# HGRN layers: state products placed between the tiles of the next values' unit, and a rearranged end of the last head pair

## The reference

```python
q, f_pre, i_in, g = split(x @ w_in)
f = lb + (1 - lb) * sigmoid(f_pre);  k = 1 - f
b = cumsum(log f)                                   # within a block
o_intra = tril(q_r @ k_r.T) @ v                     # the same block
for each block:                                     # the state goes from block to block
    o = q_inter @ state
    state = state * decay + k_state.T @ v
o = rmsnorm(o_intra + o_inter) * silu(g)
y = o @ w_out
```

## Time and profile before

| | us |
|---|---|
| median of 3 runs | 2880.5 |
| lowest and highest | 2877.11, 2885.57 |
| the profiled execution's own time | 2878.74 |
| its span, first to last instruction | 2877.0 |
| PE busy in the span | 2665.0 (93%) |
| DVE, ACT, POOL busy | 1697.5, 1300.9, 196.2 |
| TensorE's mean granted clock | 0.968 of full speed |

### The profile page before, as it was taken

How to read it: one execution, slowest core, us unless ns; L and a number is a source line. 1 busy time by engine, 2 the same in 40 slices (tenths; PEclk the granted TensorE clock), 3 DMA queues, 4 the chain that set the end, 5 groups by cost and what they waited for, 6 DMA issues and landing times.

```text
span 2877.0 us, 45279 instructions
## 1 busy us (share of the span) xinstructions
PE 2665.0 (93%) x18569; PEld 2486.4 (86%) x18569; DVE 1697.5 (59%) x1894; ACT 1300.9 (45%) x1625; POOL 196.2 (7%) x331
## 2 busy tenths in 40 slices
PE   5879989799999898999999799999799999898998
PEld 4769988699999797998989699899789999898898
DVE  6667865665555665556556655555655555575654
ACT  3644346443533554434444543444453453464543
POOL 2210002000100111000000000000010000011000
PEclk9989999899999899999999999999899999998999
DMA  8638844375555333655554355465355555443453
GB/s 289 212 125 312 333 142 147 134 243 187 190 185 187 125 118 128 201 183 179 190 175 140 109 194 185 163 204 185 130 184 187 185 181 182 153 147 103 162 190 117
DMA packets 349161, 509.52 MB, mean 177 GB/s; under 512 B 9055, under 2 KB 302118, under 8 KB 344934
## 3 DMA queue, kind: packets, MB, share of 16 engines
q1 hardware_dynamic: 343216, 493.42, 50.9%
q0 software_dynamic: 3808, 11.66, 1.1%
q10 hardware_dynamic: 2006, 2.60, 0.3%
HBM read 505.80 MB, written 1.84 MB: 176 GB/s over the span
## 4 chain that ended last, share of the span: by engine, by line
PE 83%; DVE 7%; ACT 5%; issue 2%; DMA 1%; POOL 1%; DVEq 0%; ACTq 0%; POOLq 0%
PE B L526 18%; PE B L527 18%; PE B L528 18%; PE Y L526 9%; PE Y L528 8%; PE Y L527 8%; ACT w_hi L1253 2%; DVE w_lo L1758 2%; DVE h_lo L1821 1%; ACT junk L1264 1%; DVE tmp L1783 1%; DVE x L1786 1%; DMA raw<-in_w_ada 1%; DMA raw<-in_w_in 0%; ACT h_hi L1303 0%
## 5 line engine op out<-in xcount | busy, mean ns | idle before, releaser
L1758 DVE TENSOR_TENSOR w_lo<-raw,w_hi 128x2048 fp32r<-128x2048 f32 x425 | 966.7, 2276 | 466.1 <-ACT w_hi L1253 464.8
L1253 ACT ACTIVATE w_hi<-raw 128x2048 fp32r<-128x2048 f32 x425 | 804.7, 1897 | 582.6 <-PE B L528 531.7
L526 PE MATMUL B<-h_hi,w_hi 128*128 128x256 f32 x3712 | 1053.5, 284 | 10.7 <-DVE h_lo L1821 5.9
L527 PE MATMUL B<-h_lo,w_hi 128*128 128x256 f32 x3712 | 1049.0, 283 | 0.0
L528 PE MATMUL B<-h_hi,w_lo 128*128 128x256 f32 x3712 | 1048.6, 282 | 0.0
L526 PEld LDWEIGHTS B<-h_hi,w_hi 128*128 128x128 f32 x3712 | 706.1, 190 | 16.8 <-issue 13.4
L527 PEld LDWEIGHTS B<-h_lo,w_hi 128*128 128x128 f32 x3712 | 703.5, 190 | 4.1 <-issue 0.5
L528 PEld LDWEIGHTS B<-h_hi,w_lo 128*128 128x128 f32 x3712 | 704.9, 190 | 0.0
L526 PE MATMUL Y<-w_hi,a_hi 128*128 128x512 f32 x812 | 319.3, 393 | 0.9 <-DVE M L2279 0.5
L528 PE MATMUL Y<-w_hi,a_lo 128*128 128x512 f32 x812 | 318.6, 392 | 0.0
L527 PE MATMUL Y<-w_lo,a_hi 128*128 128x512 f32 x812 | 317.6, 391 | 0.0
(11 more groups left out here) (306 smaller groups left out, 2673.2 us busy)
## 6 DMA issues: line engine op xcount, KB each, us to landing
raw<-in_ffn_w_in SPq DMA_DIRECT2D x176, 1024.0 KB, 5.1
raw<-in_ffn_w_out SPq DMA_DIRECT2D x88, 1024.0 KB, 4.9
raw<-in_w_gate_up SPq DMA_DIRECT2D x44, 1024.0 KB, 5.1
raw<-in_hgrn_w_in SPq DMA_DIRECT2D x32, 1024.0 KB, 5.3
raw<-in_w_ada SPq DMA_DIRECT2D x24, 1024.0 KB, 5.3
M<-in_w_ada SPq DMA_DIRECT2D x24, 1024.0 KB, 7.5
raw<-in_w_down SPq DMA_DIRECT2D x22, 1024.0 KB, 5.0
raw<-in_w_in SPq DMA_DIRECT2D x14, 1024.0 KB, 5.5
```

Source lines behind the costliest of these rows:

```text
L526: pe.matmul(o, lh, rh, start=first, stop=False)
L527: pe.matmul(o, lh, rl, start=False, stop=False)
L1253: act.activation(w_hi[st.n % RING][:, 0:n], raw[st.r % RING][:, 0:n], ACT.Copy).then_inc(unit_rounded, 1)
L1758: dve.tensor_tensor(w_lo[s][:, 0:n], raw[st.r % RING][:, 0:n], w_hi[s][:, 0:n].bitcast(F32), ALU.subtract).then_inc(unit_split, st.step("" ...
```

## The change

Three things are moved; no instruction is added or removed, and no size is changed.

1. On PE, the state product of pairs 0, 1 and 2 moves from the end of `scores` to the middle of the next pair's v unit, between its first and second tile. That of pair 3 stays where it was.
2. On DVE, at the end of the layer, masks and state of pair 3 come first, then `turned(0)`, and the split of the third `w_out` unit after these.
3. On PE, `turn(1)` moves from behind `out_pair(0)` into it, between its first and second tile.

```diff
-            def moving(os, name, n, lh, ll, kt, stride):
+            def moving(os, name, n, lh, ll, kt, stride, halfway=None):
                 hi, lo = unit()
                 for t in range(NT):
+                    if halfway and t:
+                        halfway()
                     for c, (o, w) in enumerate(os[t]):
...
                     mm.then_inc(tensor_step, st.step(f"{p}.far{c}"))
+
+                def state_product(c):
+                    bs = 3 if c == 3 else 7
                     pe.wait_ge(scalar_step, st.at(f"{p}.ksT{c}"))
                     pe.wait_ge(scalar_step, st.at(f"{p}.v{c}.ev"))
...
                 def out_pair(u):
+                    def before(t, i):
+                        if t == 1 and i == 0 and u == 0:
+                            turn(1)
+                        if i == 0:
+                            pe.wait_ge(vector_step, st.at(f"{p}o.h{t}.{u // 2}"))
+
...
-                    moving_unit(2, "v", c)
+                    moving_unit(2, "v", c, lambda: state_product(c - 1))
                     outputs(c - 1)
                     moving_unit(3, "g", c)
                 scores(3)
+                state_product(3)
                 turn(0)
                 outputs(3)
                 out_pair(0)
-                turn(1)
                 out_pair(2)
...
+                masked(3)
+                state(3)
+                turned(0)
                 lo(2 * D)
-                masked(3)
-                turned(0)
-                state(3)
                 gated(3)
                 normed(3)
                 turned(1)
```

More of the change, by code:

```diff
@@ L960, in stationary_unit, with moving_unit @@
                     stationary(B[u], f"{p}.{e}{c}", p if c == 0 and e == "f" else None)
-                def moving_unit(u, e, c):
+                def moving_unit(u, e, c, halfway=None):
                     if c:
                         pe.wait_ge(st.sem_of(f"{p}.{e}{c - 1}.ev"), st.at(f"{p}.{e}{c - 1}.ev"))
-                    moving([[(B[u][:, t * CH:t * CH + CH], CH)] for t in range(NT)], f"{p}.{e}{c}", CH, h_hi, h_lo, KD, CH)
+                    moving([[(B[u][:, t * CH:t * CH + CH], CH)] for t in range(NT)], f"{p}.{e}{c}", CH, h_hi, h_lo, KD, CH, halfway)
                 def scores(c):
@@ L1037, in out_pair @@
                 def out_pair(u):
+                    def before(t, i):
[3 more added lines that the diff above has]
+                            pe.wait_ge(vector_step, st.at(f"{p}o.h{t}.{u // 2}"))
                     into_y_pair(p, (f"{p}.out{u}", f"{p}.out{u + 1}"),
                                 [(h_hi[:, 2 * v:2 * v + 2, :], h_lo[:, 2 * v:2 * v + 2, :]) for v in (u, u + 1)],
-                                u == 0, u == 2,
-                                lambda t, i: None if i else pe.wait_ge(vector_step, st.at(f"{p}o.h{t}.{u // 2}")))
+                                u == 0, u == 2, before)
                 whole_input(p)
```

## The result

| | before | changed |
|---|---|---|
| median, us (runs) | 2882.35 (4) | 2839.56 (4) |
| lowest and highest | 2877.11, 2885.57 | 2838.76, 2840.19 |
| the profiled execution | 2878.74 | 2838.76 |

The ratio is 0.985, 95% interval 0.9837 to 0.9862: 42.8 us less between the medians, where 51 were forecast. 2839.56 lies in the stated range and 10.6 us over the predicted 2829. Its time is faster, as forecast; the question is where the missing 8 to 11 us are.

A forecast was written before the change was run, and what follows sets the result against it. PE fills 83% of the span, so time is won only where it waits or runs at a low clock. State product 32.4 plus layer ends 18.8 make 51.2 us off 2878.74: 2827.5, predicted as 2829 for the median, range 2820 to 2843.

The forecast's parts named there:

- State product: Pairs 0 to 2 of both HGRN layers: period 28.67 us for 34.15, 32.4 us less over six sites.
- That the clock comes back without the pause: State product and v unit behind the covered 2.9 us wait run at 1.00 instead of 0.50 and 0.69.
- The end: From turn(0) to the end of out_pair(2): 9.4 us less in each HGRN layer, 18.8 together.
- Second turn: turn(1) inside out_pair(0): PE waits 1.1 us for on3, and the 2.0 us wait before out_pair(2) goes.
- Slack of the f units' split: DVE's split for the next f unit ends 4.92 us after the v unit; PE needs it after 7.01.
- The clock falls anyway: Rival, 7%: gaps go, but the scores' many small matmuls still bring half clock for as long; 2853 us.
- the wait only moves: Rival, 4%: ksT comes as late after the first v tile as before, so part 1 gives nothing; 2862 us.
- the split of f come late: Rival, 2%, slower than before: the f unit's split collides with POOL at all six sites; 2885 us.
- block: Rival, 5%: on3 comes 3 us later, PE stands 4 us at turn(1) and the clock falls; 2838 us.
- slow stretches elsewhere that begin at another moment: Uncertainty term: slow clock after long pauses at the layers' starts begins at another moment, 2 to 3 us.
- My case: Main case, 82%: all three edits pay as worked out, 2820 to 2840 us.
- The sign that I named: PE's mean clock over the kernel up by about 0.01 from 0.968.

The follow-up runs named there:

- e1: The kernel before with only the state products of pairs 0 to 2 moved between the tiles of the v unit; median 2852.63 us, ratio 0.9906.
- e5: The kernel before with 24 idle products filling PE's wait for the keys' copy in pairs 0 to 2 of both layers; 2870.21 us, ratio 0.9962.
- e2: The kernel before with only the layer's end changed (masks and state first, second turn inside out_pair(0)); median 2863.57 us, ratio 0.9948.

## Why the prediction was right, and by how much not

- *State product.* The sum had 32.4 us; e1 alone gave 33.0, 31.9 of it in its periods. (The sum took the first site for all six; the second layer's periods before were 33.8 and 33.9, not 34.15.) The copy of the keys did stay 6.83 us behind the scores: 1002.68 - 995.85 = 6.83. The wait left was under 0.1 rather than 0.25 (PE busy 3.04 of 3.10), since the first tile took 3.0 with its last product, not 2.88.
- *That the clock comes back without the pause.* Right: 0.50 and 0.69 became 1.00, and e5 shows it with the waits left as long as they were.
- *The end.* 9.4 a layer predicted; e2 gave 9.7 and 9.4. Masks: pause 0.71, foreseen 0.8 to 1.0. Tile 0 and tile 1: 5.54 each, as worked out. Second turn: `on3` was 0.5 earlier than worked out, wait 0.56 for 1.1. `out_pair(2)` 12.43 (with the next stage's transposes) against 12.2.
- *Slack of the f units' split* (2.1 us): no new wait for it in the periods. The split beside POOL took 2.40 for 2.29.
- *Rivals.* "The clock falls anyway" and "the wait only moves" did not happen, nor did the split of f come late. `turn(1)` waited 0.56 us and the clock stayed at 1.00, so it did not block.
- *What was off* is the term "slow stretches elsewhere that begin at another moment, 2 to 3 us". I had put it into the uncertainty, either way, and small. It measured 5.4 between the layers, about twice its size, and not either way: both traces of the changed kernel had it. The 5.4 ahead of the first layer are something else: that part varied by 8 us over fourteen traces, in both kinds of kernel, ahead of everything the change touches. Whether it was chance that it fell on the changed kernel's two traces was not tested, and plain chance is doubtful. With the other parts as traced, a time of 2838 to 2840 needs an "ahead" of some 995 to 997, and seven of the changed kernel's eight runs lie there, while in all the traces together it spread from 989.6 to 997.3.
- *Sum of it.* Predicted 51.2 in the layers, measured 50.9; given back between them 5.45, and 5.4 ahead, which leaves the 40.0 between the two profiled executions. My case reached to 2840, and 2839.56 is just inside: the 10.9 us given back were several times what I had allowed for the term, and only the width left for other terms, which came out well, held them. That part is luck. The sign that I named, mean clock up by 0.01, did not come (0.968 both times), nor did the 23 us less of PE's busy time (11.8): in the layers it was 23.1, and 11.3 came back in the two unchanged parts.

What stays open is what spreads the part ahead of the first layer, and why most runs of the changed kernel gave the same time in spite of it.

## What to carry to other kernels

A short wait of TensorE can cost about twice its length: 2.9 us here brought a v unit of 7.9 for 5.75 us behind it. So fill a wait with work that is due anyway, even where that work doesn't end sooner by itself. After a change, cut both traces at the same instructions, and compare the untouched parts as well: what they gain or lose is no merit of the edit, and a delay of 1 to 2 us in front of them may turn it round. A single trace of each kernel can therefore mislead by several us.

## What had not been expected of the hardware

- The same 9564 matrix instructions between the layers took 1421.1 us in both traces of the kernel before and 1426.5 in both of the changed one; 1.66 us of idle products in the changed kernel's first layer went with 1421.4, a delay of 1.2 us in that of the kernel before with 1426.7.
- TensorE's pauses of 0.7 and 1.5 us in the changed layers left the clock at 1.00. One of 3.10 us was followed by 0.50 at once, one of 2.05 by 13.88 us at 0.88 on average, and one of 3.08 elsewhere in the same trace by 1.00.
- A POOL operation of 1.01 us took 2.98 beside a DVE split of 2.28.
